# Eight more tokens through gathered expert rows: dense expert products 376 columns wide, rows gathered as two halves of 4 KB into four buffers

## What is computed

```python
def peer(h, w_peer_q, peer_keys, peer_u, peer_v):
    q = (h @ w_peer_q).reshape(B, S, PEER_HEADS, 2, PEER_HALF)
    s = jnp.einsum('bshcd,hckd->bshck', q, peer_keys)
    sv, si = lax.top_k(s, PEER_TOPK)
    ...
    idx = jnp.take_along_axis(cidx, fpos, axis=-1)
    g = jax.nn.softmax(fv, axis=-1)
    ...
    u = peer_u[it]
    act = jax.nn.gelu(jnp.einsum('thkd,td->thk', u, xt)) * gt
    return jnp.einsum('thk,thkd->td', act, peer_v[it])
```

## Time and profile before

| | |
|---|---|
| median of 3 runs | 3885.1 us |
| the profiled execution | 3884.1 us, span 3882.3 us, granted clock 0.998 |
| PE, weight load, DVE, ACT, POOL busy | 3834.7, 3522.9, 2257.4, 1224.9, 1341.8 us |
| one `w_hi` on ACT (275) | 1896 ns, mean |
| DMA traffic | 804.19 MB, of it 268.45 MB gathered rows |
| table stage, pairs and tail | about 1778 to 1975 us, 1999 to 3873 us |

### The profile page before, as it was taken

One profiled execution on the slowest core, in us unless ns is written; L12 is line 12 of the kernel. 1 busy time (PEld: TensorE's weight loads), 2 busy tenths in 40 slices (PEclk: granted clock), 3 DMA queues, 4 the chain that ended last, 5 costly groups with the idle time before them and its releaser, 6 DMA issues.

```text
span 3882.3 us, 53851 instructions
## 1 busy us (share of the span) xinstructions
PE 3834.7 (99%) x20141; PEld 3522.9 (91%) x20141; DVE 2257.4 (58%) x3199; ACT 1224.9 (32%) x1413; POOL 1341.8 (35%) x1070
## 2 busy tenths in 40 slices
PE   7999999999999999999999999999999999999999
PEld 5778778888888878899999999999999999999999
DVE  5482552001001128886967777777767777777877
ACT  3433453333333223225642222222222222222221
POOL 0444334444444653441003333333412222222221
PEclk9999999999999999999999999999999999999999
DMA  6223112222222332334578888888888888888886
GB/s 203 87 87 107 67 55 97 97 97 97 97 97 100 137 110 93 103 121 167 207 269 319 325 312 313 330 317 317 304 302 291 308 301 312 296 300 309 293 313 230
DMA packets 165738, 804.19 MB, mean 207 GB/s; under 512 B 15504, under 2 KB 79000, under 8 KB 79512
## 3 DMA queue, kind: packets, MB, share of 16 engines
q1 hardware_dynamic: 124608, 530.62, 38.0%
q0 software_dynamic: 36864, 268.45, 18.8%
q10 hardware_dynamic: 4184, 4.01, 0.5%
HBM read 746.92 MB, written 56.10 MB: 207 GB/s over the span
## 4 chain that ended last, share of the span: by engine, by line
PE 94%; DVE 2%; issue 1%; DMA 1%; ACT 1%; POOL 0%; ACTq 0%; DVEq 0%; POOLq 0%
PE bank L1586 94%; DMA grow<-u_rows,g_col 1%; ACT w_hi L721 1%; DVE ohB L1461 1%; DVE ohA L1456 0%; PE bank L1745 0%; DVE grow L1501 0%; DVE w_lo L1442 0%; POOL w_lo L681 0%; DVE arena L1105 0%; ACT arena L721 0%; ACTq L731 0%; PE bank L1752 0%; DVE smax L1223 0%; DVE arena L1349 0%
## 5 line engine op out<-in xcount | busy, mean ns | idle before, releaser
L1586 PE MATMUL bank<-h_hi,w_hi 128*128 128x384 f32 (+1 forms) x2304 | 790.4, 343 | 9.2 <-DVE h_lo L1359 7.3
L590 POOL TENSOR_TENSOR p_lo<-ring,p_hi 128x512 fp32r<-128x512 f32 x432 | 563.4, 1305 | 673.6 <-ACT p_hi L721 588.8
L1586 PE MATMUL bank<-h_lo,w_hi 128*128 128x384 f32 (+1 forms) x2304 | 784.6, 341 | 0.0
L1586 PE MATMUL bank<-h_hi,w_lo 128*128 128x384 f32 (+1 forms) x2304 | 784.6, 341 | 0.0
L721 ACT ACTIVATE w_hi<-ring 128x2048 fp32r<-128x2048 f32 (+1 forms) x275 | 521.3, 1896 | 815.4 <-PE bank L1586 770.2
L1442 DVE TENSOR_TENSOR w_lo<-ring,w_hi 128x2048 fp32r<-128x2048 f32 x239 | 549.3, 2298 | 239.1 <-ACT w_hi L721 237.0
L1586 PE MATMUL bank<-act_hi,w_hi 128*128 128x384 f32 x2048 | 684.3, 334 | 0.5 <-DVE w_lo L1442 0.5
L1586 PE MATMUL bank<-act_hi,w_lo 128*128 128x384 f32 x2048 | 684.1, 334 | 0.0
L1586 PE MATMUL bank<-act_lo,w_hi 128*128 128x384 f32 x2048 | 684.0, 334 | 0.0
L721 ACT ACTIVATE p_hi<-ring 128x512 fp32r<-128x512 f32 x464 | 292.7, 632 | 788.8 <-PE bank L1586 784.3
L1586 PE MATMUL bank<-norm_hi,p_hi 128*128 128x512 f32 x1216 | 487.0, 400 | 1.7 <-POOL p_lo L590 1.7
(11 more groups left out here) (190 smaller groups left out, 4957.9 us busy)
## 6 DMA issues: line engine op xcount, KB each, us to landing
ring<-w_exp SPq DMA_DIRECT2D x256, 1024.0 KB
ring<-w_mix SPq DMA_DIRECT2D x64, 1024.0 KB, 4.9
gelus<-gel SPq DMA_DIRECT2D x128, 192.0 KB
tables<-wt SPq DMA_DIRECT2D x12, 2048.0 KB, 6.8
wg<-tables SPq DMA_DIRECT2D x16, 1536.0 KB, 16.7
act_in<-gelus SPq DMA_DIRECT2D x16, 1536.0 KB, 19.2
ring<-w_qk SPq DMA_DIRECT2D x20, 1024.0 KB, 4.9
ring<-w_o SPq DMA_DIRECT2D x16, 1024.0 KB, 4.9
```

The costliest lines, as they stand in the source:

```text
L590: nc.gpsimd.tensor_tensor(p_lo[:, part, :], ring[slot][:, part, :], p_hi[:, part, :].bitcast(F32), ALU.subtract).then_inc(quarter_lo, 1)
L1586: return nc.tensor.matmul(out, lhsT, rhs, start=start, stop=stop)
```

## The change

Tokens 376 to 383 leave the dense side, which becomes 376 wide (`ND`), while the tables and buffers keep 384 (`TM`). Their rows are spread over the partitions: partition 8k + t holds pairs 8k to 8k + 7 of extra token t, so that 8 more row gathers (`NX`) of u and 8 of v serve them all: 136 of each. For that, indices and weights are rearranged by 32 small DMAs of POOL, the tokens' vectors are turned by 32 matmuls inside one u tile and copied to all partitions by 16 DMAs, and at the end a selection matrix sums the 16 partial results of each token. Each gather is split in two of 4 KB a partition, into four buffers, and each dot and add into two of 1024 columns. A pair takes 20 rows, of u and of v.

```diff
-ND = S - P
+NX = 8
+NS = P // NX
+TM = S - P
+ND = TM - NX
...
-G_TURN = 6
-N_DOT = (PAIRS - JG) // G_TURN
-N_ADD = 2 * JG + 2
+ROWS_U = PAIRS + NX
+N_DOT = 2 * JG + 4
+N_LOOP = 6
+G_TURN, T_LAST, N_TURN, N_ADD = 6, 12, 3, 2 * JG + 4
...
-        g_acc = place("g_acc", 112, [KC, S])[:, :, ND:]
+        x_tok = place("x_tok", 112, [KC, S])[:, :, TM:]
+        g_acc = place("g_acc", 32, [KC, S])[:, :, TM:]
+        x_acc2 = place("x_acc2", 112, [KC, S])[:, :, TM:]
...
-        grow = [place(f"grow{i}", 180 + 8 * i, [D]) for i in range(2)]
+        grow = [place(f"grow{i}", 180 + 4 * i, [D // 2]) for i in range(4)]
...
+            pool.wait_ge(x_ready, 2)
+            for k in range(NS):
+                part, of = slice(NX * k, NX * k + NX), slice(NX * k, NX * k + NX)
+                pool.dma_start(x_idx[part, :], x_of[P - NX:, of]).then_inc(x_put, 16)
+                pool.dma_start(x_w[part, :], x_wof[P - NX:, of]).then_inc(x_put, 16)
...
+                    pool.wait_ge(gath_col, 4 * t + b + 1 + first)
+                    for half in range(2):
+                        to = 2 * (b % 2) + half
+                        pool.wait_ge(gath_free, 8 * t + 2 * b + half + 1 + 2 * first)
+                        pool.sem_inc(pool_held, 1)
+                        pool.indirect_dma_start(grow[to][:, :], None, rows,
+                                                bass.IndirectOffsetOnAxis(g_col[b][:, half:half + 1], 0)).then_inc(gath_in[to], 16)
...
+            pool.wait_ge(x_copied, 4)
+            for k in range(NS):
+                pool.dma_start(x_tok[NX * k:NX * k + NX, :, :], x_h[0:NX, :].rearrange("p (a n) -> p a n", a=KC)
+                               ).then_inc(x_spread, 16)
...
+                whole = raw[:, 0:full * TB].rearrange("p (a b) -> p a b", a=full)
+                v.tensor_tensor(whole, whole, wg[a][:, 0:full, TB * j:TB * j + TB], ALU.mult).then_inc(act_part, 1)
+                rest = raw[:, full * TB:]
+                v.tensor_tensor(rest, rest, wg[a][:, full, TB * j:TB * j + TB - NX], ALU.mult).then_inc(act_part, 1)
...
+            def a_dot(n, b, tok, sums, i):
+                for half in range(2):
+                    row = half_row(n, b, half)
+                    v.scalar_tensor_tensor(out=row, in0=row, scalar=1.0, in1=tok[:, halves[half], :], op0=ALU.mult,
+                                           op1=ALU.mult, accum_out=sums[half][:, bass.ds(i, 1)]).then_inc(gath_free, 1)
...
             def turn(g, q):
...
+                if q < T_LAST:
+                    first = N_DOT * G_TURN
+                    for i in range(first + (ROWS_U - first) * q // T_LAST, first + (ROWS_U - first) * (q + 1) // T_LAST):
+                        a_u_row(i)
+                    if q == T_LAST - 1:
+                        dve.wait_ge(gath_free, 4 + 2 * ROWS_U)
+                        v.tensor_tensor(g_dot[:, :], g_dot[:, :], g_more[:, :], ALU.add).then_inc(gath_act, 1)
+                        v.tensor_tensor(x_dot[:, :], x_dot[:, :], x_more[:, :], ALU.add).then_inc(gath_act, 1)
+                        v.memset(x_acc2, 0.0).then_inc(acc_zero, 1)
...
+            def x_tokens():
+
+                pe.wait_ge(tab_copied, 8 * NTB)
+                for c in range(KC):
+                    dst = bank[4 + c // 4][0:NX, (c % 4) * P:(c % 4 + 1) * P]
+                    mm(dst, h_hi[:, c, ND:TM], ident_r[:, :], start=True, stop=False)
+                    ins = mm(dst, h_lo[:, c, ND:TM], ident_r[:, :], start=False, stop=True)
+                ins.then_inc(x_mm, 1)
...
+            for c in range(KC):
+                ins = mm(bank[4][:, NX * c:NX * c + NX], x_acc2[:, c, :], x_sel[:, :])
+            ins.then_inc(tail_tr, 1)
```

More of the change, by code:

```diff
@@ L207, in hybrid_block @@
+        x_act = place("x_act", 200.4375, [NX])
+        x_more = place("x_more", 202.8125, [NX])
+        x_sel = place("x_sel", 202.75, [NX])
         ident_r = place("ident_r", 203, [P], F32R)
@@ new lines, in gather_all @@
+            def gather_all(first, rows, index, count, following):
+                for t in range(1 if count == 8 else 0):
+                    gather(first, rows, index, t)
+                if count > 8:
+                    with pool.Fori(0, count // 4 - 1) as t:
+                        gather(first, rows, index, t)
+                gather(first, rows, index, count // 4 - 1, following)
+            pool.wait_ge(x_copied, 4)
+            for k in range(NS):
+                pool.dma_start(x_tok[NX * k:NX * k + NX, :, :], x_h[0:NX, :].rearrange("p (a n) -> p a n", a=KC)
+                               ).then_inc(x_spread, 16)
@@ L709, in _ @@
+            pool.wait_ge(x_put, 32 * NS)
+            pool.wait_ge(x_spread, 16 * NS)
+            pool.wait_ge(x_ready, 5)
             pool.wait_ge(gath_free, 1)
             for b in range(2):
[L711 to L715, removed]
+                column(g_both, b, b)
+            gather_all(0, half_rows[0], g_both, PAIRS, x_both)
@@ L1060, in _ @@
                 high_ahead(n, n % 2)
+                if n == R_TAB + NTB:
+                    act_e.wait_ge(x_mm, 1)
+                    for b in range(4):
+                        f(x_h[0:NX, S * b:S * b + S], bank[4 + b][0:NX, :]).then_inc(x_copied, 1)
             def expert_pair(g, turn=False):
@@ L1549, in added, with a_u_row @@
-            def added(g, q):
-                extra = (2, 6)
-                i = q + sum(x < q for x in extra)
-                for more in range(1 + (q in extra)):
-                    gather_add(N_ADD * (g - G_TURN - 1) + JG + i + more, (i + more) % 2)
-            with dve.Fori(0, G_TURN) as g:
+            def a_u_row(i):
+                if i < PAIRS:
+                    dot(i, i % 2)
+                else:
+                    x_row_dot(i - PAIRS, i % 2)
+                if i == PAIRS - 1:
+                    dve.wait_ge(gath_free, 4 + 2 * PAIRS)
+                    v.memset(g_acc, 0.0).then_inc(acc_zero, 1)
@@ L1556, in _ @@
+            def added(g, q):
+                i = q + sum(x < q for x in MORE_ADD)
+                for m in range(i, i + 1 + (q in MORE_ADD)):
+                    gather_add(N_ADD * (g - G_TURN - 1) + N_TURN + m, (N_TURN + m) % 2)
+            with dve.Fori(0, N_LOOP) as g:
+                experts(g, dots)
+            for g in range(N_LOOP, G_TURN):
                 experts(g, dots)
```

188 lines of the change are left out of this document (118 added, 70 removed).

## The result

The changed kernel takes 3902.4 us (median of 6 runs, 3899.1 to 3903.9) against 3885.5 for the kernel before (6 runs): the ratio is 1.0042, with a 95% interval of 1.0031 to 1.0053. So it is slower by 17 us, by more than the 0.2% that a measurement can tell, and outside the range of 3846 to 3876. The profiled execution took 3902.9 us.

A forecast was written before the change was run, and what follows sets the result against it. PE, busy 99% of the span, was taken as the bound. The sum was 3884.1 - 39.9 + 3.5 + 1.8 + 1.5 + 0.5 = 3851.5 us, against the forecast median 3852, range 3846 to 3876.

The forecast's parts named there:

- The gain, on PE: Dense expert products: 12288 matmuls, each 3.33 ns shorter at 376 columns, save 40.9 us, net 39.9.
- is the line straight below 384?: Check on matmul spacing: any floor lies at 110 ns, far under the 170 ns wanted at 376 columns.
- the 1.0 taken off for the table stage: Table stage: 576 narrowed matmuls are only half on the chain, so 1.0 us of the gain goes back.
- Rival C: Dense matmuls: no gain per matmul, spacing stays 173.3 ns, 3892 us; chance 0.05.
- The start: Start of the pairs: 16 transfers spreading x_h delay DVE by 0.5 us, bounds 0 and 20.
- a slot of 8.15: Weighing slots on DVE: 8.1 us of work fits in 8.15, w_lo has 3.6 us of margin, cost nothing.
- Turning the extra tokens: Inside tile 44: 32 added matmuls at 0.110 us each cost PE 3.5 us, at least 2.1.
- The tail's end: End of the kernel: 16 small matmuls ahead of the transposes and one small add cost 1.8 us, bounds 1 and 4.
- The turn: Change from dot to adding pairs: DVE makes w_lo late, PE waits 1.5 us, bounds 0 and 8.
- rival B: Pairs: gathered rows come late; mild form 3858 to 3876 us, chance 0.17; hard form 3942, chance 0.09.
- The forecast for halves: Row gathers in the pairs: half a row lands sooner than a whole, an argument against late rows; no size given.

The follow-up runs named there:

- experiment 2: Kernel before with only its dense products narrowed to 376 columns, leaving out the expert products of 8 tokens: 3884.1 us, ratio 0.9999.
- experiment 5: Changed kernel without the 16 transfers; DVE repeats the extra tokens' columns so matmuls fill all partitions: 3894.2 us, ratio 1.0022 to the kernel before.
- experiment 1: Separate kernel without the layer, 96 bare matmuls per width, each with a 128-column weight load: 173.3 ns each at 384 and 376 columns.

## Why the prediction was wrong

**The gain, on PE: this step failed, and with it the sign.** "Eight columns are then 3.33 ns" took the straight line between 384 and 512 down to 376. The rows behind it were right, and so was the count of 12288, but no row was 376 wide, and the check "is the line straight below 384?" asked only for a floor: it found that 128 columns take 0.110 us and took all between for a line. The bare matmuls show 173.3 ns at 376 as at 384, and experiment 2 shows it in the kernel: -39.9 became 0, with the 1.0 taken off for the table stage. The slope itself was sound, for 368, 336, 320 and 256 columns lie on that line; what failed is the step from a line through some widths to a price for every width.

**Rival C named the outcome with the wrong reason.** "Spacing stays 173.3 ns: 3892" had 0.05, "for it only the 188 ns load". The spacing stayed, but not by the load, which lets 344 columns go every 153 ns. What should have raised its chance: a spacing known at two widths says nothing of a third, and the two ends known, 0.110 us at 128 and 173.3 at 384, do not lie on the line of 0.416 ns a column (that would give 67 at 128); so the line was known to break somewhere between, and I had no row that said where. The bare matmuls put that break below 256 columns (120.0 ns, on the line), so it is not what failed at 376: that this width lies off the line could be found only by timing it.

**The start was priced by the wrong time.** I priced the 16 transfers by their issue, 0.965 to 1.1 us each, and they were issued sooner than that. They cost 10.0 us and not 0.5, by landing late and holding up the weight tiles beside them: no bound of mine was about the other traffic, and 10 lies between the bounds of 0 and 20 by luck. Without them 9.7 us are back by 2050 us (experiment 5). Who shares the DMA engines with them was not asked, with the DMA engines at 0.84 to 0.86 in the pairs already.

**The tail was not a slot of the kind that I weighed.** The 8.1 us in a slot of 8.15 came from a dot pair's slot, "without slack", and "I cost it at nothing". In the tail a weighing slot also adds to `xT` and takes a `gather_add`, and it measured 8.33 before and 8.58 after, so DVE falls behind in each; and a slot with two rows follows, whose last half was 3.65 us late. Nothing in the sum for it, 5.7 us measured.

**Small terms.** Turning the extra tokens: 3.5 predicted, 2.0 measured, since with 8 columns of weights the 128-wide matmuls go every 60 ns; just under the lower bound of 2.1. The tail's end: 1.8 predicted and 1.8 measured, but by luck and not by my working. The timeline of PE at the end, after:

```profile
3890.45 3.63 PE L1705 MATMUL bank<-x_sel,x_acc 128*128 128x8 f32 x32
3893.93 1.94 PE L2133 MATMUL bank<-ident,g_acc 128*128 128x128 f32 x16
```

The 16 small products are 32 on PE and take 3.5 us, twice what I gave them. DVE's last add so ends 6.8 us behind the last dense matmul, in place of 3.8; of these 3.0 us 1.2 come back at the output, since the first store goes out (at 3891.7 us) while PE is at the small products, and the last one is issued at once behind its add, not 1.2 us later as before. The turn: 1.5 predicted, 0.7 measured. PE's gap there is 0.76 us from start to start, of the kind predicted.

**Rows late (rival B), in either form, did not come in the pairs.** The DMA share is 0.87 to 0.88, the waits for rows fell, and the adding pairs cost nothing. The one late half that counts lies in the tail. The forecast for halves, "half a row lands sooner than a whole", was right.

Summed with what was measured: 3884.1 + 0.3 + 2.0 + 10.0 - 1.7 + 0.7 + 5.7 + 1.8 = 3902.9, the profiled execution's time.

## What to carry to other kernels

Before narrowing an operation that repeats twelve thousand times, time the exact width by itself: a slope between two widths is no price for a third, and the gain that one width does not give may lie a few columns further (374 in the bare stream, 368 in the kernel). Price a one-off transfer by when it lands and by what shares the DMA engines, not by its issue; if PE and ACT can produce the copy, the engines stay free. When an engine is said to have room, look for its fullest slot in every stage, since work taken from one stage (the tail here) comes back as stalls in another.

## What the hardware showed that I had not expected

- The spacing of matmuls that each load 128 columns of weights is uneven in the width: 384, 378 and 376 columns all 173.3 ns, 374 169.3, 368 166.7, 344 and 336 both 153.3, 256 120.0, and 111.7 from 224 down to 128 (experiment 1). Eight of the 21 widths above the floor lie on columns / 2.4 + 13.3 ns, 376 lies 3.3 ns above it. 376 alternates between 170 and 177 ns.
- With weights of only 8 columns, 128-wide matmuls go every 60 ns (the changed kernel), against 110 to 112 with 128 columns of weights (experiment 1).
- A wait of PE of 3.2 us was followed by steps of 313 ns, 376 columns at 1.2 GHz, so that it cost 5.1 us in all; the wait at the turn, 0.76 us from start to start, shows no such steps.
- Sixteen small transfers from 8 partitions to 128, 1 MB together, took 6.8 to 23.1 us each to land, and used the DMA engines at 6.0 KB a us; the chain waited 23 us for a weight tile beside them, where the median of such tiles is 5.7 in the page of the changed kernel.
